# Retention in a two-block transformer on one core: value products in three passes, gates in another buffer, narrower query panels

## The reference

```
q, k : 256 features   v, g : 512 features          (all from h @ w_in)
scores(t, s) = (q_t . k_s / 16) * gamma^|t-s|       where s's chunk of 64 is not after t's
o_t = sum_s scores(t, s) * v_s
y   = silu(g) * o / sqrt(mean(o^2) + 1e-6)          then y @ w_out
```

## Time and profile before

| | |
|---|---|
| time, median of 3 runs | 2737.88 us (2737.18 to 2741.91) |
| span of the profiled execution | 2738.4 us |
| instructions | 39302 |
| TensorE, VectorE, ScalarE, GpSimd busy | 98%, 47%, 37%, 10% |
| value products (L909) | 160 matmul records, 782.8 to 1113.4 us |
| moved by transfers | 232.93 MB, mean 85 GB/s |

### The profile page before, as it was taken

How to read it: one execution, slowest core, us unless ns; L and a number is a source line. 1 busy time by engine, 2 the same in 40 slices (tenths; PEclk the granted TensorE clock), 3 DMA queues, 4 the chain that set the end, 5 groups by cost and what they waited for, 6 DMA issues and landing times.

```text
span 2738.4 us, 39302 instructions
## 1 busy us (share of the span) xinstructions
PE 2684.4 (98%) x16240; PEld 2339.2 (85%) x16240; DVE 1288.2 (47%) x2198; ACT 1019.6 (37%) x1621; POOL 276.8 (10%) x350
## 2 busy tenths in 40 slices
PE   8999999999999999999999999999999999999997
PEld 7888999999988878788888988888888887988887
DVE  4664654333542423573344533435666664633333
ACT  4654433222432223352223432323566543522222
POOL 0000300001200000220000310012211130300002
PEclk9999999999999999999999999999999999999998
DMA  4111243222111212232222232222322222232320
GB/s 141 55 47 47 78 139 104 91 90 81 55 62 62 93 62 81 89 109 93 95 97 93 73 127 93 85 95 76 108 85 70 74 82 85 85 108 93 100 70 31
DMA packets 67682, 232.93 MB, mean 85 GB/s; under 512 B 9008, under 2 KB 11440, under 8 KB 67120
## 3 DMA queue, kind: packets, MB, share of 16 engines
q1 hardware_dynamic: 67504, 230.41, 25.8%
HBM read 228.25 MB, written 2.10 MB: 84 GB/s over the span
## 4 chain that ended last, share of the span: by engine, by line
PE 89%; DVE 3%; ACT 3%; POOL 2%; issue 2%; DMA 1%; SPq 0%; DVEq 0%; POOLq 0%; ACTq 0%
PE ps L606 78%; PE ps L909 2%; POOL R L2740 1%; PE ps L1038 1%; PE ps L616 1%; PE ps L808 1%; PE ps L768 1%; PE ps L896 1%; POOL S L2725 1%; ACT HT L1286 1%; DVE HT L1961 1%; DVE R L1968 1%; PE ps L1114 1%; PE ps L1135 1%; PE ps L626 0%
## 5 line engine op out<-in xcount | busy, mean ns | idle before, releaser
L606 PE MATMUL ps<-XH,LENT 128*128 128x512 f32 (+2 forms) x2448 | 608.4, 339 | 2.8 <-DVE XL L1985 2.7
L606 PE MATMUL ps<-HH,LENT 128*128 128x264 f32 (+2 forms) x2292 | 508.6, 318 | 3.8 <-DVE LENT L1934 1.9
L606 PE MATMUL ps<-XH,WH 128*128 128x264 f32 (+2 forms) x1680 | 489.0, 332 | 13.7 <-DVE XL L2699 7.9
L606 PE MATMUL ps<-XL,WH 128*128 128x264 f32 (+2 forms) x1680 | 475.9, 324 | 0.0
L606 PE MATMUL ps<-XH,WL 128*128 128x264 f32 (+2 forms) x1680 | 475.5, 324 | 0.0
L606 PEld LDWEIGHTS ps<-XH,LENT 128*128 128x128 f32 x2448 | 411.9, 188 | 60.2 <-issue 3.8
L606 PEld LDWEIGHTS ps<-HH,LENT 128*128 128x128 f32 x2292 | 371.8, 189 | 36.1 <-DVE HL L1941 2.7
L606 PE MATMUL ps<-XL,LENT 128*128 128x512 f32 (+2 forms) x1224 | 381.0, 339 | 0.0
L1934 DVE TENSOR_TENSOR WL<-RAW,WH 128x1024 fp32r<-128x1024 f32 (+1 forms) x214 | 263.4, 1232 | 207.8 <-ACT WH L1242 207.6
L1934 DVE TENSOR_TENSOR LENT<-RAW,LENT 128x1024 fp32r<-128x1024 f32 (+1 forms) x210 | 261.5, 1252 | 185.6 <-ACT LENT L1242 185.4
L606 PE MATMUL ps<-HL,LENT 128*128 128x264 f32 (+2 forms) x1146 | 340.2, 317 | 0.0
(11 more groups left out here) (222 smaller groups left out, 2647.6 us busy)
## 6 DMA issues: line engine op xcount, KB each, us to landing
RAW<-in_wf SPq DMA_DIRECT2D x128, 512.0 KB, 3.3
RAW<-in_wr SPq DMA_DIRECT2D x48, 512.0 KB, 3.3
RAW<-in_wg SPq DMA_DIRECT2D x44, 512.0 KB, 3.2
RAW<-in_wu SPq DMA_DIRECT2D x44, 512.0 KB, 3.3
RAW<-in_wd SPq DMA_DIRECT2D x32, 512.0 KB, 3.3
RAW<-in_we SPq DMA_DIRECT2D x24, 512.0 KB, 3.4
RAW<-in_wm SPq DMA_DIRECT2D x24, 512.0 KB, 3.3
RAW<-in_wro SPq DMA_DIRECT2D x16, 512.0 KB, 3.3
```

Of the source, the lines that this page charges most:

```text
L606: mm = e.matmul(o[:, to:to + m], wt, xt[:, k, c0 + a * m:c0 + (a + 1) * m], start=(n == 0 and j == 0), stop=(n == nk - 1 and j == 2))
```

## The change

Three parts. The value products become three passes of fp32r matmuls over high and low halves of the turned values (`r_VT`, now a pair) and of the decayed scores (`r_STH`, `r_STL`); ScalarE makes the scores' high half, VectorE the low one in place of the f32 scores, and for the values VectorE subtracts the high half that ScalarE has copied. The scores are packed (`ST_AT`) to the 1536 columns that are used. The gates, for which no scratch is left, are written to `GATE`, which is the memory of `HL`. And the query panels of heads 1 to 3 run over the 512 real tokens instead of all 528 columns. With the values' end (`RET_VALUES`) moved from 7312 to 10304, two more `LENT` slots may be filled after the last value product.

```diff
+ST_AT = list(itertools.accumulate((TW - q for q in FIRST_Q), initial=0))
+N_ST = ST_AT[-1]
...
+    with nc.sbuf_tensor("GATE", [P, 8, TW], F32) as GATE:
+        pass
     HL = sb("HL", [P, 8, TW], F32R)
...
-    r_VT = scr(5 * 512).rearrange("p (j c) -> p j c", j=5)
-    r_ST = scr(5 * TW).rearrange("p (j c) -> p j c", j=5)
+    r_VT = [LENT[:, scr.skip(5 * 512):scr.at].rearrange("p (j c) -> p j c", j=5) for _ in range(2)]
+    st_at = scr.skip(2 * N_ST)
+    r_ST = SCR[:, st_at:st_at + N_ST]
+    r_STL, r_STH = LENT[:, st_at:st_at + N_ST], LENT[:, st_at + N_ST:st_at + 2 * N_ST]
+    RET_VALUES = scr.at
     r_O = [scr(512) for _ in range(4)]
-    r_G = [scr(512) for _ in range(4)]
+    def r_G(h, f):
+        return GATE[:, 4 * (h % 2) + f, NM:TW]
...
@@ lent_ready @@
-            if PLACE[i][1] + 2048 <= 7312:
+            if PLACE[i][1] + 2048 <= RET_VALUES:
                 return S.value["ret", 3, 3]
...
@@ tensor: ret_head @@
-                w.wait_ge(*S.decayed[h, 4])
+                w.wait_ge(*S.st_lo[h, 4])
                 w.wait_ge(*S.vt_act["ret", h, 3])
                 w.wait_ge(*S.vt_dve["ret", h, 3])
                 for j, (k0, kn) in enumerate(KB):
-                    lo = FIRST_Q[j]
-                    mm = e.matmul(o[:, lo - NM:512], r_VT[0:kn, j, f * 128:f * 128 + 128], r_ST[0:kn, j, lo:TW],
-                                  start=(j == 0), stop=(j == 4))
+                    lo, (a, b) = FIRST_Q[j], ST_AT[j:j + 2]
+                    for n, (vt, st) in enumerate(((r_VT[0], r_STH), (r_VT[0], r_STL), (r_VT[1], r_STH))):
+                        mm = e.matmul(o[:, lo - NM:512], vt[0:kn, j, f * 128:f * 128 + 128], st[0:kn, a:b],
+                                      start=(j == 0 and n == 0), stop=(j == 4 and n == 2))
@@ tensor: ret_qk (and ret_q(2 * h + i, NM, 512, None) on ScalarE) @@
-                drain(gemm("wr", idx, X, x_ready("ln01", None), 0, TW, (S.q_copy, "ret", AT["wr", idx], None), beside=beside))
+                drain(gemm("wr", idx, X, x_ready("ln01", None), NM, 512, (S.q_copy, "ret", AT["wr", idx], None), beside=beside))
@@ scalar: ret_head, behind the last ret_turn_v @@
+            for j, (k0, kn) in enumerate(KB):
+                w.wait_ge(*S.decayed[h, j])
+                a, b = ST_AT[j:j + 2]
+                e.activation(r_STH[0:kn, a:b], r_ST[0:kn, a:b], ACT.Copy).then_inc(*S.st_hi(h, j))
...
-                if h == 0:
-                    w.wait_ge(*lent_back("ret"))
-                else:
-                    w.wait_ge(*S.scaled["ret", h - 1, f])
-                e.activation(r_G[f], val(("panel", AT["wr", idx], None), 512), ACT.Silu).then_inc(*S.silu("ret", h, f))
+                w.wait_ge(*H_free(f"ret{h // 2}"))
+                e.activation(r_G(h, f), val(("panel", AT["wr", idx], None), 512), ACT.Silu).then_inc(*S.silu("ret", h, f))
@@ vector: ret_turn_v @@
-            e.tensor_copy(r_VT[0:16, 4, f * 128:f * 128 + 128],
-                          acc(("ret_v", h, f), 2)[0:16, 512:640]).then_inc(*S.vt_dve("ret", h, f))
+            v, cols = acc(("ret_v", h, f), 2), slice(f * 128, f * 128 + 128)
+            hi, lo = r_VT
+            e.tensor_copy(hi[0:16, 4, cols], v[0:16, 512:640]).then_inc(*S.vt_tail(h, f))
+            w.wait_ge(*S.vt_act["ret", h, f])
+            e.tensor_tensor(lo[:, 0:4, cols], v[:, 0:512].rearrange("p (j c) -> p j c", j=4), hi[:, 0:4, cols].bitcast(F32),
+                            ALU.subtract)
+            w.wait_ge(*S.vt_tail[h, f])
+            e.tensor_tensor(lo[0:16, 4, cols], v[0:16, 512:640], hi[0:16, 4, cols].bitcast(F32),
+                            ALU.subtract).then_inc(*S.vt_dve("ret", h, f))
@@ vector: ret_head @@
             for f in range(4):
                 drain(ah.steps("wr", 32 + 4 * h + f))
+                if f == 0:
+                    ret_lower(h, 0, 2)
+                if f == 1:
+                    ret_lower(h, 2, 5)
...
+        def ret_lower(h, first, end):
+            for j in range(first, end):
+                kn, (a, b) = KB[j][1], ST_AT[j:j + 2]
+                w.wait_ge(*S.st_hi[h, j])
+                e.tensor_tensor(r_STL[0:kn, a:b], r_ST[0:kn, a:b], r_STH[0:kn, a:b].bitcast(F32),
+                                ALU.subtract).then_inc(*S.st_lo(h, j))
```

More of the change, by code:

```diff
@@ L321, in __call__, with skip @@
         def __call__(self, n):
-            a = self.at
+            a = self.skip(n)
+            return SCR[:, a:a + n]
+        def skip(self, n):
             self.at += n
             assert self.at <= NSCR, self.at
-            return SCR[:, a:a + n]
+            return self.at - n
     scr = Carve()
@@ L343, in build_program @@
     r_k = [scr(TW) for _ in range(2)]
-    r_VT = scr(5 * 512).rearrange("p (j c) -> p j c", j=5)
-    r_ST = scr(5 * TW).rearrange("p (j c) -> p j c", j=5)
+    r_VT = [LENT[:, scr.skip(5 * 512):scr.at].rearrange("p (j c) -> p j c", j=5) for _ in range(2)]
[3 more added lines that the diff above has]
+    RET_VALUES = scr.at
     r_O = [scr(512) for _ in range(4)]
-    r_G = [scr(512) for _ in range(4)]
+    assert scr.at <= RET_KEPT
+    def r_G(h, f):
+        return GATE[:, 4 * (h % 2) + f, NM:TW]
     DT = TAB[:, 0:2304].rearrange("p (a b) -> p a b", a=4)
@@ L464, in build_program @@
     S.rms, S.scaled = signal("rms"), signal("scaled")
+    S.st_hi, S.st_lo, S.vt_tail = (signal(n) for n in ("st_hi", "st_lo", "vt_tail"))
     S.square, S.decayed, S.out_copy = signal("square"), signal("decayed"), signal("out_copy")
@@ L1553, in ret_turn_v @@
                 w.wait_ge(*S.value["ret", h - 1, 3])
-            e.activation(r_VT[:, 0:4, f * 128:f * 128 + 128],
+            e.activation(r_VT[0][:, 0:4, f * 128:f * 128 + 128],
                          acc(("ret_v", h, f), 2)[:, 0:512].rearrange("p (j c) -> p j c", j=4),
@@ L1600, in ret_qk @@
                 drain(ah.steps("wr", 2 * h + i, beside=beside))
-                ret_q(2 * h + i, 0, TW, None)
+                ret_q(2 * h + i, NM, 512, None)
                 if i == 0:
@@ L2312, in ret_head @@
                     w.wait_ge(*S.value["ret", h - 1, 3])
-                e.tensor_tensor(r_ST[0:kn, j, TW - n:TW], acc(("ret_s", h, j), 1)[0:kn, 0:n], DT[0:kn, h, 48 + TW - n - k0:48 + TW - k0],
+                e.tensor_tensor(r_ST[0:kn, ST_AT[j]:ST_AT[j + 1]], acc(("ret_s", h, j), 1)[0:kn, 0:n], DT[0:kn, h, 48 + TW - n - k0:48 + TW - k0],
                                 ALU.mult).then_inc(*S.decayed(h, j))
@@ L2348, in ret_out @@
                 w.wait_ge(*S.gated["ret", h, f])
-                e.tensor_tensor(r_O[f], r_G[f], roots, ALU.mult).then_inc(*S.scaled("ret", h, f))
+                e.tensor_tensor(r_O[f], r_G(h, f), roots, ALU.mult).then_inc(*S.scaled("ret", h, f))
                 w.wait_ge(*S.scaled["ret", h, f])
@@ L2781, in gpsimd @@
                 w.wait_ge(*S.out_copy[h, f])
-                e.tensor_tensor(r_G[f], r_G[f], r_O[f], ALU.mult).then_inc(*S.gated("ret", h, f))
+                e.tensor_tensor(r_G(h, f), r_G(h, f), r_O[f], ALU.mult).then_inc(*S.gated("ret", h, f))
         down_norm("ln10")
```

## The result

The changed kernel takes 2732.22 us (median of 20 runs, 2729.27 to 2735.56) where the kernel before takes 2736.86 in 20 runs. The ratio is 0.9983, 95% interval 0.9977 to 0.9989: 4.6 us faster, between 3.0 and 6.3. Forecast was 2731.4 with a range of 2726.5 to 2735.8; measured from the later median of before, the forecast saving of 6.5 us would give 2730.4. The gain is 0.17%. The prediction gave 0.62 to a gain of over 0.2% and 0.34 to what came, a time within 0.2% of before.

What follows compares the result with a forecast made beforehand. TensorE, busy 98% of the span, was taken to bound the kernel, so only time off its queue or waits counts: 2737.9 - 5.3 (value products) - 1.2 (query panels) = 2731.4 us, range 2726.5 to 2735.8.

Steps and rivals of the forecast that it cites:

- The value products: Retention stage: fifteen fp32r records a block instead of ten f32 ones, 2.70 us a block against 3.03, 5.3 us saved.
- 16-row product: Last key block's narrow value product: 0.64 us a block in three passes, where f32 took 0.56.
- Rival (a): Value products: the count of passes alone sets time, a quarter less, 12.1 us saved, 2724.6 with the panels; chance 0.08.
- Rival (c): Value products: weight loads stay bare in all fifteen records, 3.77 us a block, slower at 2748.5 us; chance 0.04.
- (b): Small end: wide records pace at 0.24 us, narrow product 0.70; 2.7 + 0.8 us saved, 2734.4 us; chance 0.22.
- The 0.56 us: Time of the f32 16-row product in a 3.03 us block, beside 2.47 us for the four wide products.
- The query panels: Heads 1 to 3: six panels save 0.25 us each, less some 0.1 us wait a head; 1.2 us saved.
- The added work at nothing: Added VectorE subtractions and ScalarE copies beside TensorE cost nothing, covered by over 10 us at the nearest place.
- rival (d): Splits behind the new copies come late, costing 0 to 2.2 us a head; 2731 to 2740 us; chance 0.04.
- The two more slots: LENT slots that may be filled after the last value products instead of after the last output half: zero cost.
- The sum: Whole kernel: 5.3 and 1.2 us saved pass through whole, 2737.9 to 2731.4 us.
- What was to be seen: Trace signs: 240 fp32r records, 10.7 us a head, idle about 0.2 us around 16-row loads, 0.1 us sum-of-squares wait.

Runs made afterwards that it cites:

- padded kernel: The changed kernel with the last key block's value product over 128 rows instead of 16, the added rows zero: 2729.14 us, ratio 0.9974 to the kernel before.
- the padding in f32: The kernel before, value products still f32, with only the last key block's product over 128 rows instead of 16: 2732.38 us, ratio 0.9983.
- queries_only: The kernel before with only the query panels of heads 1 to 3 over 512 columns instead of 528: 2735.97 us, ratio 0.9996.
- control: The kernel before, run again unchanged: 2735.98 us, ratio 1.0002.

## Why the prediction was right, and where it was off

**The value products:** 2.70 us a block forecast. The piece of the chain is 10.58 us a head for 10.7, and saves 1.35 us a head, 5.4 in all for 5.3. The wide part holds: from start to start the trace has 0.23 us a record at 512 columns, 0.20 at 448, 0.146 at 320 and about 0.11 at 192. What a block of 10.58 / 4 us leaves beside the forecast's 2.06 is 0.59 for the 16-row product, for 0.64, and the padded kernel takes 0.25 of it away. Rival (a), the count of passes alone (12.1 us), is out. The count is right but is no price even where only columns move: three passes of 512 columns take 3 x 0.234 = 0.70 us where the f32 product took 0.86, a fifth less and not a quarter; the products of 192 columns gain nothing (0.33 for 0.32), and the narrow one gets no shorter. Rival (c), bare loads, is out, and so is (b) with 2.86 us a block.

One reading under this term was wrong. The load side does not stand idle 0.24 us behind the narrow product: that idle time of the earlier trace rows belongs to the next block's wide loads (see the padding in f32), and the hold behind the narrow product shows only as a step of 0.25 us between loads. The 0.56 us came from a difference of block and wide products and did not need it, so the sum stands.

**The query panels:** 1.2 forecast, 1.16 in the stage. The wait for VectorE came as described, but at about 0.2 us a head instead of 0.1 (1.08 us for 0.86), and the panels gave 0.6 us a head instead of 0.5 (queries_only). That the sum of the two came out to 0.04 us is luck: the two errors cancel.

**The added work at nothing:** right. The turned block's subtractions end 1.55 us behind the turn for 1.6 forecast, the last of the scores' 13 us before the products for 12, and the cover held value subtractions and score copies of three times the length; rival (d) is out. Moving the gates: nothing, as forecast. The two more slots: ScalarE's first split behind the last head starts 1128.04 - 1113.51 = 14.53 us after the end of the products before and 1120.71 - 1106.20 = 14.51 now, so the tail is unchanged.

**The sum:** the stage gives 6.52 us for 6.5, the time 4.6. What was wrong is the step that the saving comes out at the end whole: 1.7 us are lost again inside the span, mostly in the memory attention by the traces, and 0.3 outside it. The forecast allowed a microsecond or two either way for the clock behind 1140 us, in its last paragraph; it did not put it into the chance of "faster", where 0.62 was too much for a forecast that lay 1 us from the bound.

**What was to be seen:** the 240 records, the piece of 10.7 and the unchanged waits are there. The idle time of about 0.2 us on both sides of the 16-row loads is not: the steps of 0.29 and 0.23 us between loads leave 0.10 and 0.04 us beside a load's recorded 0.19, which the timeline merges. The wait of about 0.1 us in front of the sum of squares came as 0.2.

## What to carry to other kernels

Price a three-pass product by what each pass is bound by: its columns when wide, and at 192 columns already its weight load, 0.11 us for 128 columns. Before trading passes, look for a product with fewer rows between full ones: filling its operands with zeros to 128 rows gave as much here (0.9983) as the whole change, and 3 to 4 us more on top of it. When a trace says a stage is shorter by some microseconds and the medians say less, profile the unchanged kernel again, and then compare the spans of all runs: here one pair of traces could not tell chance from a loss, and some hundred runs could.

## What was not expected of the hardware

A product of 16 or 32 rows between products of 128 costs 0.25 to 0.3 us more than the same product over 128 rows (10.58 against 9.57 us a head in three passes, 11.93 against 10.73 in f32). It lies in the change of rows, for three 16-row loads in a row keep the step of 0.11 us. And two executions of one program differ by 5 us in span (2738.4 and 2733.4) while 374 us of nearly uninterrupted TensorE work in them agree to 0.01. Of the 5 us, 2.4 lie in front of the retention stage, where the granted clock of before is 0.89 from 45 to 60 us and 0.83 from 310 to 330 us and the control's 1.00 and 0.91, and 2.5 behind it.
